# Gate projections of a SwiGLU by Strassen's seven block products, in a four-layer decoder trunk on one core

## What is computed

```
def swiglu_ffn(h, w_gate, w_up, w_down):
    return (jax.nn.silu(h @ w_gate) * (h @ w_up)) @ w_down
```

## Time and profile before

| | |
|---|---|
| median of 3 runs | 2778.58 us (2777.53 to 2778.63) |
| the profiled execution | 2777.52 us |
| its span, first to last instruction | 2775.8 us |
| TensorE busy | 2763.9 us, 14344 matmuls |
| VectorE, ScalarE, GpSimd busy | 1354.9, 1021.0, 610.4 us |

### The profile page before, as it was taken

The page is one execution under the profiler, slowest core; times in us unless marked ns, Lnnn a source line. Parts: engine busy times, 40 slices in busy tenths (PEclk is TensorE's granted clock), DMA queues, the critical chain, the costliest instruction groups (busy, mean ns, idle before and its releaser), DMA issues. The chain is left out here.

```text
span 2775.8 us, 37592 instructions
## 1 busy us (share of the span) xinstructions
PE 2763.9 (100%) x14344; PEld 2322.1 (84%) x14344; DVE 1354.9 (49%) x1889; ACT 1021.0 (37%) x1637; POOL 610.4 (22%) x506
## 2 busy tenths in 40 slices
PE   9999999999999999999999999999999999999999
PEld 7888888888888888888888888888888888888888
DVE  4464543345668663333655555543335464543333
ACT  5332432225257552322443443432224332432222
POOL 0021322203113442220321121322202022322211
PEclk9999999999999999999999999999999999999999
DMA  5323233333620123333322223233333333233331
GB/s 170 91 84 92 81 102 99 96 100 108 169 62 2 42 81 106 91 104 95 107 88 81 77 83 99 82 101 97 93 97 111 88 91 87 73 109 100 91 97 65
DMA packets 448359, 256.08 MB, mean 92 GB/s; under 512 B 9728, under 2 KB 431984, under 8 KB 448112
## 3 DMA queue, kind: packets, MB, share of 16 engines
q1 hardware_dynamic: 446944, 251.69, 31.3%
q10 hardware_dynamic: 1296, 2.75, 0.3%
HBM read 248.11 MB, written 2.10 MB: 90 GB/s over the span
## 5 line engine op out<-in xcount | busy, mean ns | idle before, releaser
L1808 DVE SCALAR_TENSOR_TENSOR w_lo<-w_raw,w_hi 128x1024 fp32r<-128x1024 f32 x461 | 635.4, 1380 | 848.3 <-ACT w_hi L1350 847.5
L601 PE MATMUL acc<-a_hi,w_hi 128*128 128x512 f32 (+1 forms) x2136 | 835.8, 391 | 0.3 <-DVE g_lo L2245 0.3
L603 PE MATMUL acc<-a_hi,w_lo 128*128 128x512 f32 (+1 forms) x2136 | 829.0, 388 | 0.0
L602 PE MATMUL acc<-a_lo,w_hi 128*128 128x512 f32 x1944 | 756.6, 389 | 0.0
L1350 ACT ACTIVATE w_hi<-w_raw 128x1024 fp32r<-128x1024 f32 x460 | 483.3, 1051 | 524.2 <-PE acc L603 468.7
L603 PEld LDWEIGHTS acc<-a_hi,w_lo 128*128 128x128 f32 x2136 | 401.1, 188 | 82.9
L601 PEld LDWEIGHTS acc<-a_hi,w_hi 128*128 128x128 f32 x2136 | 401.3, 188 | 82.3 <-DVE g_lo L2245 1.2
L602 PEld LDWEIGHTS acc<-a_lo,w_hi 128*128 128x128 f32 x1944 | 365.2, 188 | 74.5 <-issue 1.0
L603 PE MATMUL acc<-hid_hi,w_lo 128*128 128x512 f32 (+1 forms) x704 | 264.5, 376 | 0.0
L602 PE MATMUL acc<-hid_lo,w_hi 128*128 128x512 f32 (+1 forms) x704 | 264.5, 376 | 0.0
L601 PE MATMUL acc<-hid_hi,w_hi 128*128 128x512 f32 (+1 forms) x704 | 264.5, 376 | 0.0
(11 more groups left out here) (387 smaller groups left out, 3713.9 us busy)
## 6 DMA issues: line engine op xcount, KB each, us to landing
w_raw<-ffn_w_gate SPq DMA_DIRECT2D x88, 512.0 KB, 3.8
w_raw<-ffn_w_up SPq DMA_DIRECT2D x88, 512.0 KB, 3.8
w_raw<-gm_w_in SPq DMA_DIRECT2D x64, 512.0 KB, 4.1
w_raw<-ffn_w_down SPq DMA_DIRECT2D x64, 512.0 KB, 3.8
w_raw<-ret_w_in SPq DMA_DIRECT2D x48, 512.0 KB, 3.8
w_raw<-gm_w_out SPq DMA_DIRECT2D x32, 512.0 KB, 3.8
w_raw<-ffn_w_down SPq DMA_DIRECT2D x32, 384.0 KB, 3.4
w_raw<-nsa_w_in SPq DMA_DIRECT2D x21, 512.0 KB, 4.2
```

Source lines behind the costliest of these rows:

```text
L601: pe.matmul(o_bank, lhs_hi, rhs_hi, start=start, stop=False)
L602: pe.matmul(o_bank, lhs_hi, rhs_lo, start=False, stop=False)
L603: return pe.matmul(o_bank, lhs_lo, rhs_hi, start=False, stop=stop)
L1808: dve.scalar_tensor_tensor(w_lo[:, slot, :, :], w_raw[:, slot, :, :], 1.0, w_hi[:, slot, :, :].bitcast(f32), ALU.mult, ALU.subtract).then_ ...
```

## The change

In groups 3 to 9 of each layer (`SEVEN_FROM`, `SEVEN_TO`) the two gate units, a matrix of 1024 x 256 against 1024 x 512 activations, are cut into 2 x 2 blocks on both sides and multiplied by seven block products instead of eight (Strassen's scheme in its form with shared sums). A block product is 4 row tiles of 128 x 128 weights against 256 tokens: 12 matmuls of 256 columns into half a bank of `tr` or `st`. The two up units of the group stay as they were. Units are now in the order gate, gate, up, up.

What is new around it: GpSimd makes four sums of weight blocks per group (`weight_sums`), 128x512 each, and ScalarE and VectorE split them (`sums_high`, `sums_low`); of the two gate units only the blocks that stand in a product by themselves are split, so unit 1 of the pair is split in its lower half alone. The four sums of token blocks are made once per layer: ScalarE writes `a_full` in group 1, GpSimd sums it, and both splits follow in group 2 (`tokens_high`, `tokens_low`). ScalarE copies one block product out of `st`; VectorE joins the seven in four additions and scales both gate tiles by R at once (`join`). SiLU and the product with up work on both tiles together (`gated_pair`). GpSimd's product is written to `hid_full`, which shares its place with `hid_lo`, and the splits of the hidden tiles move from the loop to group 10: ScalarE rounds all 22, VectorE makes the first 14 low parts (`LOW_BY_VECTOR`), GpSimd the other 8. The loads of a gate pair wait for the sums of the pair before (`s_sum`). In the first and fourth layer's mixer some semaphores are merged (`v_agg` into `v_stat`, four `ws_` ones into two), without another order of work.

```
 ENTRY = 3
+SEVEN_FROM, SEVEN_TO = 3, 10
+SEVENS = SEVEN_TO - SEVEN_FROM
+LOW_BY_VECTOR = 14
...
+        def unit_rows(i, j):
+
+            return slice(DT // 2, DT) if j == 2 and is_seven(i + 1) else slice(0, DT)
...
-                stream(L["n_up"], 11, 4,
-                       lambda i, j: cols((ffn_w_gate if j % 2 == 0 else ffn_w_up)[l], 0, D_MODEL, i * (2 * P) + (j // 2) * P), ONE)
+
+                def up_group(i):
+                    for j in range(4):
+                        slot = (L["n_up"] + j) % SLOTS
+                        src = cols((ffn_w_gate if j < 2 else ffn_w_up)[l], 0, D_MODEL, i * (2 * P) + (j % 2) * P)
+                        if j >= 2 or (isinstance(i, int) and i <= SEVEN_FROM):
+                            load(i * 4 + (L["n_up"] + j), slot, src, DT)
+                            continue
+                        sp.wait_ge(s_sum, sums_base(L, i))
+                        sp.dma_start(w_raw[:, slot, :, :], src.rearrange("(k p) m -> p k m", p=P)).then_inc(loaded[slot], 16)
...
+                def seven(i):
+                    slot0, slot1 = n0 % SLOTS, (n0 + 1) % SLOTS
+                    if isinstance(i, int):
+                        pe.wait_ge(r_ready, L["b_mid"] + 1)
+                    else:
+                        pe.wait_ge(acc_free, i * 4 + (o0 - 2))
+                    for r, (k, out_half, t) in enumerate([(0, tr[:, 1, first], 0), (2, tr[:, 1, second], 2), (1, st[:, 0, second], 1), (3, tr[:, 0, second], None)]):
+                        pe.wait_ge(s_lo, sums_base(L, i) + (r + 1))
+                        rhs_hi = a_hi[:, bottom, second] if t is None else t_hi[:, t, :, :]
+                        rhs_lo = a_lo[:, bottom, second] if t is None else t_lo[:, t, :, :]
+                        block_product(out_half, s_hi_of[k], s_lo_of[k], rhs_hi, rhs_lo).then_inc(s_used, 1)
+                    pe.wait_ge(lo_done, i * 4 + (n0 + 1))
+                    block_product(st[:, 1, first], w_hi[:, slot0, top, :], w_lo[:, slot0, top, :], a_hi[:, top, first], a_lo[:, top, first]).then_inc(s_used, 1)
+                    block_product(st[:, 0, first], w_hi[:, slot0, bottom, :], w_lo[:, slot0, bottom, :], a_hi[:, bottom, first], a_lo[:, bottom, first]).then_inc(unit_done, 1)
+                    pe.wait_ge(lo_done, i * 4 + (n0 + 2))
+                    block_product(tr[:, 0, first], w_hi[:, slot1, bottom, :], w_lo[:, slot1, bottom, :], t_hi[:, 3, :, :], t_lo[:, 3, :, :]).then_inc(unit_done, 1)
+                    for j in range(2, 4):
+                        plain_unit(i, j)
+
+                entry(L["b_mid"])
+                for i in range(1, SEVEN_FROM):
+                    for j in range(4):
+                        plain_unit(i, j)
+                seven(SEVEN_FROM)
+                with pe.Fori(0, SEVENS - 1) as r:
+                    seven(r + (SEVEN_FROM + 1))
...
+                def sums_high(i):
+
+                    for r, k in enumerate((0, 2, 1, 3)):
+                        act.wait_ge(s_sum, sums_base(L, i) + (r + 1))
+                        act.activation(s_hi_of[k][:, :, :], s_full_of[k][:, :, :], ACT.Copy).then_inc(s_hi, 1)
...
+                def plain(i):
+                    if i == 1:
+                        for t in range(DT):
+                            last = act.activation(a_full[:, t, :], h[:, t, :], ACT.Copy, scale=gain[:, gain_of(L["b_mid"]), t:t + 1])
+                        last.then_inc(p1_out, 1)
+                    if i == 2:
+                        tokens_high()
                     for j in range(4):
                         if not begun_split(i, j):
-                            ahead(L["n_up"], i, 4, j)
-                        p, q = j // 2, i * 2 + (L["q_up"] + j // 2)
-                        if j % 2 == 0:
...
-                            act.wait_ge(hid_mul, q + 1)
-                            act.activation(hid_hi[:, i * 2 + p, :], work[:, 2 * p, :], ACT.Copy).then_inc(hid_hi_done, 1)
-                loop(act, 11, swiglu, 1)
+                            ahead(n0, i, 4, j, unit_rows(i, j))
+                        if i == SEVEN_TO and j < 3:
+                            hid_high(*[(0, LOW_BY_VECTOR), (LOW_BY_VECTOR, 2 * SEVEN_TO - 2), (2 * SEVEN_TO - 2, 2 * SEVEN_TO)][j])
+                        if j < 2:
+                            act.wait_ge(acc_free, i * 4 + o0 + j + 1)
+                            act.activation(work[:, j, :], work[:, j, :], ACT.Silu).then_inc(silu_done, 1)
...
+                def seven(i):
+                    last = isinstance(i, int) and i == SEVEN_TO - 1
+                    ahead(n0, i, 4, 0)
+                    act.wait_ge(s_used, used_base(L, i) + 5)
+                    act.activation(sq[:, 0, 0:HALF], st[:, 1, 0:HALF], ACT.Copy).then_inc(p1_out, 1)
+                    ahead(n0, i, 4, 1)
+                    ahead(n0, i, 4, 2, unit_rows(i, 2))
+                    if not last:
+                        sums_high(i + 1)
+                    act.wait_ge(m_step, i * 4 + (SEVENS * 4 * L["layer"] - 4 * SEVEN_FROM + 4))
+                    act.activation(work[:, 0:2, :], work[:, 0:2, :], ACT.Silu).then_inc(silu_done, 2)
+                    ahead(n0, i, 4, 3)
+                    if last:
+                        act.wait_ge(unit_done, n0 + 4 * i + 2)
...
+                def sums_low(i):
+
+                    for r, k in enumerate((0, 2, 1, 3)):
+                        if k < 2:
+                            dve.wait_ge(s_sum, sums_base(L, i) + (3 if k == 0 else 4))
+                        dve.wait_ge(s_hi, sums_base(L, i) + (r + 1))
+                        dve.scalar_tensor_tensor(s_lo_of[k][:, :, :], s_full_of[k][:, :, :], 1.0, s_hi_of[k][:, :, :].bitcast(f32),
+                                                 ALU.mult, ALU.subtract).then_inc(s_lo, 1)
...
+                def plain(i):
+                    if i == 2:
...
                     for j in range(4):
                         if not begun_split(i, j):
-                            ahead(L["n_up"], i, 4, j)
-
-                        if j % 2 == 0:
-                            wait(dve, hid_lo_done, i * 2 + (L["q_up"] + j // 2 - 1))
-                        leave(i * 4 + (L["n_up"] + j), work[:, j, :], (L["o_up"] + j) % BANKS, R[:, :])
-                loop(dve, 11, swiglu, 1)
+                            ahead(n0, i, 4, j, unit_rows(i, j))
+                        if i == 2 and j == 2:
+                            sums_low(SEVEN_FROM)
+                        if i == SEVEN_TO and j == 0:
+                            for t in range(LOW_BY_VECTOR):
+                                dve.wait_ge(hid_hi_done, q0 + t + 1)
+                                dve.scalar_tensor_tensor(hid_lo[:, t, :], hid_full[:, t, :], 1.0, hid_hi[:, t, :].bitcast(f32),
+                                                         ALU.mult, ALU.subtract).then_inc(hid_lo_done, 1)
+                        wait(dve, hid_mul, q0 + (2 * SEVEN_TO if i == SEVEN_TO else 2 * i - 1 + j % 2))
...
+                def join(i):
+
+                    step = i * 4 + (SEVENS * 4 * L["layer"] - 4 * SEVEN_FROM)
+                    low, both = tr[:, :, :].rearrange("p a n -> p (a n)"), work[:, 0:2, :]
+                    dve.wait_ge(hid_mul, i * 2 + q0)
+                    dve.wait_ge(p1_out, p1_count(L, i))
+                    dve.wait_ge(unit_done, i * 4 + (n0 + 1))
+                    dve.tensor_tensor(both[:, :, 0:HALF], by_side(st[:, 0, :]), sq[:, 0, 0:HALF].unsqueeze(1).broadcast_to([P, 2, HALF]), ALU.add).then_inc(m_step, 1)
+                    dve.wait_ge(m_step, step + 1)
+                    dve.tensor_tensor(both[:, :, HALF:SEQ], by_side(tr[:, 1, :]),
+                                      work[:, 1, 0:HALF].unsqueeze(1).broadcast_to([P, 2, HALF]), ALU.add).then_inc(m_step, 1)
+                    dve.wait_ge(unit_done, i * 4 + (n0 + 2))
+                    dve.wait_ge(m_step, step + 2)
+                    dve.tensor_tensor(work[:, 1, 0:HALF], tr[:, 0, 0:HALF], work[:, 1, HALF:SEQ], ALU.add).then_inc(m_step, 1)
+                    dve.wait_ge(m_step, step + 3)
+                    dve.tensor_tensor(both[:, :, HALF:SEQ], by_side(low[:, HALF:3 * HALF]), both[:, :, HALF:SEQ], ALU.add).then_inc(acc_free, 2)
+                    dve.wait_ge(acc_free, i * 4 + (o0 + 2))
+                    dve.tensor_tensor(both, both, R[:, :].unsqueeze(1).broadcast_to([P, 2, SEQ]), ALU.mult).then_inc(m_step, 1)
+
+                def seven(i):
+                    ahead(n0, i, 4, 0)
+                    ahead(n0, i, 4, 1)
+                    ahead(n0, i, 4, 2, unit_rows(i, 2))
+                    join(i)
+                    if not (isinstance(i, int) and i == SEVEN_TO - 1):
+                        sums_low(i + 1)
+                    leave(i * 4 + (n0 + 2), work[:, 2, :], (o0 + 2) % BANKS, R[:, :])
+                    ahead(n0, i, 4, 3)
...
+
+                for i in range(SEVEN_FROM):
...
+                def weight_sums(i):
+
+                    slot0, slot1 = n0 % SLOTS, (n0 + 1) % SLOTS
```

(86 more changed lines are left out.)

130 lines of the change are left out of this document (89 added, 41 removed).

## The result

| | before | after |
|---|---|---|
| median of 4 runs | 2778.6 us (2777.53 to 2778.63) | 2757.09 us (2755.8 to 2758.99) |
| profiled execution | 2777.52 us | 2755.80 us |
| its span | 2775.8 us | 2753.8 us |

The ratio is 0.9924, 95% interval 0.9907 to 0.9941. Between the two profiled executions lie 21.72 us; forecast were 22.8.

What follows compares the result with a forecast made beforehand. TensorE, which never stands, was taken as the bound. 28 groups × 0.81 us = 22.8 us off 2778.58 gave 2755.8 us, with joins, sums, waits, turn-in and late split at 0; range 2752.5 to 2763 us.

Steps and rivals of the forecast that it cites:

- TensorE's part: Gate units in groups 3 to 9: 84 narrow matmuls replace 48 wide, gaining 0.81 us a group, 22.8 us in all.
- the two up units stay at 10.88: Up units after the block products keep their 10.88 us, so a group goes from 21.76 to 20.95 us.
- The first term: The seven block products of a group: 84 matmuls of 256 columns at 0.1198 us, 10.07 us.
- The median: Median of the runs, taken as 1.06 us above the profiled execution: 2778.58 − 22.8 = 2755.8 us.
- Sequencer: TensorE's sequencer: seven waits, 0.7 to 1.4 us of issuing a group, hidden by a 2.1 us lead; cost 0.
- Rival D: TensorE's queue fails to cover register waits before narrow matmuls: 33.6 us lost against 22.8 gained, 2789 us; chance 0.06.
- The seven's deadlines: Joins, sums and splits in a steady group cost 0; first sum's low part ready at 17.6, wanted 20.95, 3.3 us spare.
- Rival C: VectorE and GpSimd exclude each other on SBUF work, so the gain is gone: 2773 to 2784 us; chance 0.04.
- Turn-in: Each layer's groups before the first block products, with token sums and first weight sums: cost 0, margins 4.8 to 8 us.
- late split: Splitting hidden tiles in group 10 before the down projection: cost 0, margins 5.7 to 6.4 us.

## Why the prediction was right

**TensorE's part.** The mechanism, 28 groups each shorter with TensorE never standing, was right to the matmul count. The term mis-sized is "the two up units stay at 10.88": they take 10.90, because the first five wide matmuls behind narrow ones cost 0.03 us more together. 28 × 0.78 = 21.8 us, measured 21.72 between the profiles. The first term, 84 × 0.1198 = 10.07, was measured as 10.08 (84 steps from 2472.97). One number beside the sum was mixed up: 1.36 us is an eighth of the whole price of 48 matmuls, with six fixed parts in it. The columns alone are worth 6 × 0.2138 = 1.28 us, and the 36 more fixed parts of 0.0129 take 0.46 back. The forecast of 0.81 didn't use it.

**The median.** 2755.8 was forecast, 2757.09 and 2758.82 measured in two sets of 4 and 5 runs, both inside the range. The first profile's execution, at 2755.80, is among the fastest. The profile of the kernel run again has the same 218.9 us from entry to down projection in the last layer; its last entry is 1.8 us later, 1.2 of it already at the end of the first entry. Adding 1.06 us for the median, as before, was too little by 0.2 us in the first set and by some 2 in the second; what makes the opening vary wasn't tried.

**Sequencer.** Right that it costs nothing, and right about the cover: the lead of 2.1 us is also what stands ahead of the fifth block of a seven, with and without the extra waits. Rival D is refuted further than the changed kernel alone does: eight more waits ahead of each block, none of them seen. The fear that 1.4 us of waits "eats most of that lead" was too dark, because the waits are spread over seven blocks and the lead is made good between them. Ahead of a seven's first block, where wide matmuls stand in front, the wait is executed at 2469.1 and the first matmul starts at 2472.97, 3.8 us later. As an estimate from both rows (2.14 / 0.12 and 3.8 / 0.227) the lead is some 17 or 18 matmuls and not a fixed time.

**The seven's deadlines.** First low part ready at 16.2 and not at 17.6: the join starts at 11.7, where I had 12.3, and takes 3.9 us with its handshakes, where I had 4.6. So 4.8 us of slack and not 3.3. It was tested: 3.34 us of delay were free, about 7.6 were not.

**Exclusive lock.** Rival C was right on the mechanism and wrong on its price: a w_lo behind a pair takes 3.27, 1.09 us of its own after the pair's end at 2497.43. By the Trainium skill, "SBUF — State Buffer", section "Who interferes with whom", a VectorE instruction with two SBUF inputs contends with a GpSimd instruction that reads SBUF, and the trace agrees. The lock accounts for part of the busy times over forecast (VectorE's 38 us, GpSimd's 56): the one blocked sum in each of six groups a layer makes 24 × 0.98 = 24 of the 56, and the three of the turn-in another 3 us a layer, 12 in all. But in a seven it falls in the first 6 us, where nobody waits.

**Turn-in and late split.** Unit 5's w_lo came 1.6 us earlier, forecast 1.9. The first weight sums' low parts are ready near 2448 and wanted at 2452, 4 us ahead where 4.8 were forecast. In the late split the order was right and the lock was missing from my sum. VectorE's 14 tiles end at G+13.3 (forecast 12.3), GpSimd's six low parts took 10.04 us in place of 7.8. The two rows are the changed kernel's, with G = 2598.86:

```profile
2615.00 10.04 POOL L2823 TENSOR_TENSOR hid_lo<-hid_full,hid_hi 128x512 fp32r<-128x512 f32 x6 [12.39 <-ACT hid_hi L1895]
...
2630.31 1.30 POOL L2823 TENSOR_TENSOR hid_lo<-hid_full,hid_hi 128x512 fp32r<-128x512 f32 x1 [0.74 <-ACT hid_hi L1895]
```

Tile 21 is ready at 2631.61, wanted at 2620.61 + 21 × 0.68 = 2634.9: 3.3 us to spare, not 6.4. That it isn't on the path is shown by four sevens gaining as much each as seven do, and by the down projection, 121.05 us before and after.

## What to carry to other kernels

When an algorithm saves multiplications but makes them narrower, price both widths from distances of starts in a stream: here an eighth of the columns was worth 1.28 us a group, 36 more fixed parts took 0.46 back and the dearer first wide ones 0.03, so the gain was 0.78. Then treat every other engine as a list of deadlines, and put beside each the engine that it shares a lock with: a margin worked out from durations alone shrank from 6.4 to 3.3 us, and with one more group it was gone. Where GpSimd's result is due, try a pause in VectorE's row: without one, one more group of Strassen was worth nothing here; with one and earlier splits together it was worth its full 0.8 us a layer. Last, when you read how far a sequencer runs ahead, find the product that a wait belongs to by its line, not by its time.
